# Branch products of a hybrid encoder layer: order of copies, splits and loads around them

## The chip, the cores and the metric

The kernel runs on one core of one Trainium2 chip, as one program. The metric is the device time of the program in microseconds. Three runs of the kernel before are known: 1832.99, 1835.6 and 1838.12 us, so the median is 1835.6 us. One more execution was profiled.

## The reference, cut to what matters

One layer on 512 frames of 2048 channels, all in float32. After a layer norm, one projection feeds three attention branches and their gates:

```
branches = (oa * silu(ag), ob * silu(bg), oc * silu(cg))        # each 512 x 1024
for n in range(3):
    gate = sigmoid(mg[..., n*2048:(n+1)*2048] + b_gate[n])      # 512 x 2048
    merged += gate * (branches[n] @ w_branch[n])                # 512 x 1024 @ 1024 x 2048
y = merged @ w_out
out = layer_norm(2**0.25 * h + y)
```

The change lies around the three products `branches[n] @ w_branch[n]`, and in one load of the last product `merged @ w_out`.

## The kernel before, in words

Every float32 product is made of three matmuls on parts of its operands. A value is split into a high part (ACT copies it to the format fp32r) and a low part (DVE subtracts the high part from the value); TensorE adds low x high, high x low and high x high in PSUM. Weights are split in the kernel as well, so each chunk of weights passes this way: SP issues its load into a slot of `raw` (4 slots of 512 KB), ACT writes `w_hi` (`split_hi`, L1262), DVE writes `w_lo` (`split_lo`, L1842), TensorE uses it (12 matmuls of 128x512), and the slot goes on. `split_hi(c)` and `split_lo(c)` work on chunk c + 3 (`LOOKAHEAD`); ACT waits in it until chunk c - 1 is multiplied, SP's load of a chunk waits until the low part of the chunk 4 before it is written.

**The gate groups** (L898 to L955, L1480, L2195) come before the branch products. In the last of them (group 7) DVE makes sums of weights in place of the weights (`weight_sum`, L2002). The fourth sum of a row of tiles is the last that reads `w_11`, which lies on the same bytes as `raw`. Behind group 7 the first chunks of the branch products are split between its last pieces (L1511, L2222).

**The branch products** use two forms. Branches 2 and 1 go through `halved_group` (L1141): 4 groups (s = 0 to 3), each one half of the columns of a branch, each with 7 products G1, G5, G6, G2, G7, G3, G4 in place of 8 (the Strassen-Winograd scheme), 2 chunks each, so 14 chunks a group. G5, G6, G7 and G4 take sums of weights that GpSimd's accumulating DMAs have made in DRAM (`t_dram`); the others take `w_branch` itself. The partial results stay in three pairs of PSUM banks, z, y and x. Before TensorE may start on a bank again something has to leave it: ACT copies z after G1, y after G5 and z after G6 (`copy_halved`, L1713, at steps j = 2, 4, 6); DVE adds x at j = 8, z at j = 10 and y at j = 12 (`add_out`, L2024). G6, G7 and G3 wait for the three copies, G4 for the add at j = 10, the next group for the other two (L1145 to L1157). DVE then multiplies by the gates (`halved_gates`, L2455, at j = 9, 11, 13; `halved_21`, L2473, at the next group's j = 0). ACT makes the tanh of two gate blocks a group (`gate_tanh`, L1708), which GpSimd loads from DRAM, 1 MB each (`load_gate`, L3027).

Branch 0 goes through plain products: 4 column blocks m of 4 chunks (L1171), with its own split tiles `bra_hi` and `bra_lo` (`branch_hi` L1475, `branch_lo` L2177), 8 tiles k of 128x512. TensorE needs tile k of them when it comes to the k-th of 8 parts of block m = 0.

The unsplit branches 1 and 0 come back from DRAM in one load of 2 MB each (`load_branch`, L2895), issued by GpSimd between its gate loads (L3040 to L3057). GpSimd issues in program order, so a load behind a wait waits too.

The order on ACT and DVE is written out by hand, step j by step j, as in

```python
                for j in range(STEPS):
                    split_hi(CH_M + STEPS * s + j)
                    ...
                    if j == 6:
                        copy_halved(s, 6, z, u2_buf, ev_u2, 6)
                        gate_tanh(2 * s)
```

**The output product** (L1201, L2692, L3070) uses the same scheme on `w_out`, with quarters of it in `w_x`, `w_y` and `w_z`. SP loads the quarters (`load_out`, L661); GpSimd adds further quarters into them with accumulating DMAs of 512 KB (`sum_out`, L3059), each as soon as the piece it overwrites is split. The order of TensorE's first pieces is G1 and G3, then G5 (from `w_x` after the adds), then G2 (from `w_z`, the third quarter), G6, G7, G4. SP issues the four loads of the third quarter once piece (G3, 1) is split (L674).

Of the kernel before, what the change touches and what calls it, by code (L numbers as in the profile page):

```python
# [31 lines left out]
D = 2048  # L32
# [6 lines left out]
BT = BW // P  # L39
# [15 lines left out]
RING = 4  # L55
# [13 lines left out]
CH_M = CH_A + 4 * PAIRS  # L69
# [28 lines left out]
SUMMED_C, SUMMED_B = 6, 8  # L98
SUMMED = 2 * (SUMMED_C + SUMMED_B)
LEFT_SUMS = 5  # L100
TOEP_DONE = 16 + 16 * PAIRS
# [9 lines left out]
def t_index(g, t, k):  # L111

    return 4 * BT * g + BT * (t - 1) + k
# [71 lines left out]
def program(nc, x, mem, ln_in_g, ln_in_b, rel_table, w_in, b_gate, b_forget, sinks,  # L185
# [205 lines left out]
    with ExitStack() as ctx:  # L391
# [146 lines left out]
        def _(sp):  # L538
# [107 lines left out]

            sp.wait_ge(t_ready, t_index(GROUPS, 1, 0))
            sp.wait_ge(toep_stored, TOEP_DONE + 16 * 8 * HALVED)
            for s in range(HALVED):
                for p in range(PRODUCTS):  # L650
                    src = t_dram[s, RIGHT[p]] if p in (G5, G6, G7, G4) else branch_weights(2 - s // 2, s % 2, RIGHT[p])
                    for h in range(2):
                        c = CH_M + STEPS * s + 2 * p + h
                        load(c, c % RING, src[2 * h * P:2 * (h + 1) * P, :].rearrange("(k p) n -> p k n", p=P), 2)
            for m in range(D // 512):
# [9 lines left out]
            def split_done(g, p, d):  # L665
                sp.wait_ge(pc_lo, OUT_BASE + double(g, p, d) + 1)
# [5 lines left out]
            for d in range(DOUBLES):  # L672
                load_out("22", w_y, 0, 1, 1, d)
            split_done(0, G3, 1)  # L674
            for d in range(DOUBLES):
# [585 lines left out]
        def _(act):  # L1261
# [197 lines left out]
            def halved_hi(b, p):  # L1459

                if p in (G5, G6, G7, G3):
                    made_at = {G5: 1, G7: 2, G6: 3, G3: 5}[p]
                    act.wait_ge(m_summed, LEFT_SUMS * b + made_at)
                else:
                    act.wait_ge(br_loaded[2 - b], 16)
                if b:
                    act.wait_ge(multiplied, CH_M + STEPS + 2 * p + 2)
                elif p in (G5, G6, G3):
                    act.wait_ge(pc_lo, piece(GROUPS - 1, G4, 2 * (G5, G6, G3).index(p) + 2))
                else:  # L1470
                    act.wait_ge(pc_mult, piece(GROUPS - 1, G4, 0))
                pick = branch_tiles(p)
                act.activation(pick(br_hi, bs_hi), pick(br_raw[b], bs_raw[b]), ACT.Copy).then_inc(br_hi_ready, 1)

            def branch_hi(k):  # L1475

                act.wait_ge(br_loaded[0], 16)
                act.activation(bra_hi[:, k, :], bra_raw[:, k, :], ACT.Copy).then_inc(br_hi_ready, 1)
# [240 lines left out]
            for s in range(HALVED):  # L1719
                z, y, x = gate_banks(GROUPS + s)  # L1720
                for j in range(STEPS):
                    split_hi(CH_M + STEPS * s + j)
                    if s == 0 and j < 4:
                        halved_hi(0, G2 + j)
                    if s == 0 and j == 6:
                        act.wait_ge(st_c12, 16 * GROUPS)
                    if j == 2:
                        copy_halved(s, 2, z, p1_buf, ev_s1, 2)
                    if j == 4:
                        copy_halved(s, 4, y, p5_buf, ev_s5, 4)  # L1730
                    if j == 6:
                        copy_halved(s, 6, z, u2_buf, ev_u2, 6)
                        gate_tanh(2 * s)
                    if j == 8:
                        gate_tanh(2 * s + 1, -0.5)
                    if s == 1 and j and j % 2 == 0:
                        halved_hi(1, j // 2 - 1)
                    if s == 2 and j == 0:
                        halved_hi(1, G4)
                    if s == 3 and j >= 12:  # L1740
                        branch_hi(j - 12)

            last_m = D // 512 - 1
            for m in range(last_m + 1):
                for s in range(4):
# [3 lines left out]
                    split_hi(CH_PLAIN + 4 * m + s)  # L1749
                    if m == 0 and s < 3:  # L1750
                        branch_hi(2 * s + 2)
                        branch_hi(2 * s + 3)
                    if s == (0 if m else 2):
# [87 lines left out]
        def _(dve):  # L1841
# [304 lines left out]
            def halved_sum(b, n):  # L2146
# [4 lines left out]
                if n:  # L2151
                    dve.wait_ge(m_summed, LEFT_SUMS * b + n)
                else:
                    dve.wait_ge(br_loaded[2 - b], 16)
                if n == 0:
# [329 lines left out]
            for s in range(HALVED):  # L2485
                g = GROUPS + s
                z, y, x = gate_banks(g)
                for j in range(STEPS):
                    if j == 10:
                        job_done(CH_M + STEPS * s + 9)  # L2490
                        dve.wait_ge(ev_s5, 2 * g + 2)
                        add_out(z, p5_buf, ev_c22)
                    split_lo(CH_M + STEPS * s + j)
                    if s == 0 and j < 5:
# [4 lines left out]
                    if s and j == 0:  # L2499
                        halved_21(s - 1)  # L2500
                    if j == 8:
                        job_done(CH_M + STEPS * s + 7)
                        dve.wait_ge(ev_s1, 2 * g + 2)
                        add_out(x, p1_buf, ev_c11)
                    if j == 9:
                        dve.wait_ge(ev_c11, 2 * g + 2)
                        halved_gates(s, 0, 0, p1_buf, 1.0)
                    if j == 11:
                        dve.wait_ge(ev_c22, 2 * g + 2)
                        halved_gates(s, 1, 1, p5_buf, -1.0)  # L2510
                    if j == 12:
                        job_done(CH_M + STEPS * s + 11)
                        dve.wait_ge(ev_u2, 2 * g + 2)
                        add_out(y, u2_buf, ev_c12)
                    if j == 13:
# [6 lines left out]
                    if s == 2 and j in (1, 2, 3, 4):  # L2522
                        halved_lo(1, G2 + j - 1)
                    if s == 3 and j >= 12:
                        branch_lo(j - 12)

# [56 lines left out]
            for m in range(last_m + 1):  # L2583
                for s in range(4):
# [3 lines left out]
                    if m == 0 and s == 0:  # L2588
                        halved_21(HALVED - 1)
                    if m == 0 and s < 3:  # L2590
                        branch_lo(2 * s + 2)
                        branch_lo(2 * s + 3)
                    if m == last_m - 1 and s == 1:
# [197 lines left out]
        def _(pool):  # L2791
# [103 lines left out]
            def load_branch(n, dst):  # L2895
                if n == N_BRANCH - 1:
                    pool.wait_ge(br_stored, 16 * (HC + 2 * PAIRS))
                pool.dma_start(dst, br_dram[n].rearrange("k p n -> p k n")).then_inc(br_loaded[n], 16)

            def store_gate(g, half_n, half_t, buf, done):  # L2900
                n, nb = N_BRANCH - 1 - (g - KV_GROUPS) // 2, 2 * (g % 2) + half_n
# [142 lines left out]
            store_gate(GROUPS - 1, 0, 1, s1_buf, st_c21)  # L3044
            load_gate(1)
            pool.wait_ge(multiplied, CH_M + 4)
            load_branch(1, br_raw[1][:, :, :])
            for done in (st_c11, st_c22, st_c21):
                pool.wait_ge(done, 16 * GROUPS)
            for m in range(2, 6):  # L3050
                load_gate(m)
            pool.wait_ge(multiplied, CH_M + 2 * STEPS + 6)
            load_branch(0, bra_raw[:, :, :])
            for m in range(6, 2 * HALVED + D // 512):
                load_gate(m)
                if m >= 2 * HALVED:
                    pool.dma_start(out_t[m - 2 * HALVED], ln_b[0].partition_broadcast(P)).then_inc(preset, 16)  # L3057
# [120 lines left out]
```

## Time and profile before

| | us |
|---|---|
| three runs | 1832.99, 1835.6, 1838.12 |
| the profiled execution, its own time | 1833.84 |
| its span, first to last instruction | 1832.1 |
| TensorE busy | 1807.1 |
| VectorE (DVE) busy | 1345.8 |
| ScalarE (ACT) busy | 902.7 |
| GpSimd busy | 240.6 |
| mean granted TensorE clock, share of full | 0.997 |

Times in the profile are microseconds from the first instruction. A matmul of 512 columns is shown as 0.39 us long, but the next starts 0.227 us after it; its end is modelled, and it overlaps the next. What TensorE loses is therefore read from the distance of starts, or from the idle time in brackets. Group 7's G4 runs from 1394 to 1406.6 us, the four groups of the branch products from 1406.8 to 1562.9, the plain products of branch 0 from 1565 to 1661, the output product from there to 1819.

### The profile page before, as it was taken

How to read it: one execution, taken by the hardware profiler on the slowest of the kernel's cores; microseconds unless marked ns; L12 is line 12 of the kernel's file. 1: busy time of each engine (PE TensorE's matmuls, PEld its weight loads, DVE VectorE, ACT ScalarE, POOL GpSimd, SP SyncE). 2: the span in 40 equal slices, each digit the busy share in tenths (PEclk: the TensorE clock that was granted, in tenths of full speed). 3: DMA queues.
4: the chain of work that ended last, by engine and by line, in shares of the span. 5: the costliest groups of instructions: out<-in, count | busy, mean ns of one | idle time of the engine just before them, and what ended most of it. 6: DMA issues, size and time to landing. Idle time of an engine off the chain costs nothing.

```text
span 1832.1 us, 24225 instructions
## 1 busy us (share of the span) xinstructions
PE 1807.1 (99%) x8481; PEld 1496.9 (82%) x8481; DVE 1345.8 (73%) x2130; ACT 902.7 (49%) x1504; POOL 240.6 (13%) x308
## 2 busy tenths in 40 slices
PE   9999999999999999999999999999999999999997
PEld 7888888888888888888888888888887887787885
DVE  5777774887777776566678877878788777656778
ACT  5653332545555554344445545545456575344543
POOL 1111110100222221001101110101111000002222
PEclk9999999999999999999999999999999999999999
DMA  9576676962765544355566967858787877739987
GB/s 329 184 204 176 188 199 208 247 218 59 197 199 151 180 130 141 110 154 158 122 191 179 263 152 193 234 124 235 182 229 184 313 258 251 247 133 201 240 209 178
DMA packets 249640, 354.98 MB, mean 194 GB/s; under 512 B 14480, under 2 KB 141520, under 8 KB 245968
## 3 DMA queue, kind: packets, MB, share of 16 engines
q1 hardware_dynamic: 178352, 200.83, 34.6%
q0 software_dynamic: 71056, 152.50, 34.3%
q8 instruction: 50, 0.82, 0.2%
q10 hardware_dynamic: 144, 0.52, 0.1%
q14 instruction: 38, 0.31, 0.1%
HBM read 303.30 MB, written 97.11 MB: 219 GB/s over the span
## 4 chain that ended last, share of the span: by engine, by line
PE 87%; DVE 5%; DMA 4%; ACT 1%; issue 1%; POOL 0%; DVEq 0%; POOLq 0%; SPq 0%; ACTq 0%
PE acc L715 10%; PE acc L717 10%; PE acc L716 10%; PE scores L906 6%; PE scores L910 6%; PE scores L908 6%; PE acc L910 3%; PE acc L906 3%; PE acc L908 3%; PE transposed L740 3%; DMA raw_weights<-anch_weight_sums_scratch 2%; PE attended L910 2%; PE attended L906 2%; PE attended L908 2%; DVE w_lo L1853 2%
## 5 line engine op out<-in xcount | busy, mean ns | idle before, releaser
L1380 ACT ACTIVATE piece_split<-w 128x512 fp32r<-128x512 f32 x448 | 282.5, 632 | 289.8 <-PE scores L910 105.6
L1999 DVE TENSOR_TENSOR piece_split<-w,piece_split 128x512 fp32r<-128x512 f32 x448 | 309.2, 691 | 108.3 <-ACT piece_split L1380 97.8
L1853 DVE TENSOR_TENSOR w_lo<-raw_weights,w_hi 128x1024 fp32r<-128x1024 f32 x205 | 249.3, 1221 | 149.8 <-ACT w_hi L1275 148.0
L715 PE MATMUL acc<-h_hi,w_lo 128*128 128x512 f32 x800 | 319.2, 399 | 0.0
L717 PE MATMUL acc<-h_hi,w_hi 128*128 128x512 f32 x800 | 312.5, 391 | 0.0
L716 PE MATMUL acc<-h_lo,w_hi 128*128 128x512 f32 x800 | 311.7, 390 | 0.0
L1275 ACT ACTIVATE w_hi<-raw_weights 128x1024 fp32r<-128x1024 f32 x205 | 216.1, 1059 | 158.1 <-PE acc L717 27.3
L717 PEld LDWEIGHTS acc<-h_hi,w_hi 128*128 128x128 f32 x800 | 150.1, 188 | 32.2
L715 PEld LDWEIGHTS acc<-h_hi,w_lo 128*128 128x128 f32 x800 | 150.4, 188 | 30.0 <-issue 1.8
L716 PEld LDWEIGHTS acc<-h_lo,w_hi 128*128 128x128 f32 x800 | 150.6, 188 | 28.5
L906 PE MATMUL scores<-piece_split,h_lo 128*128 128x512 f32 x384 | 150.2, 391 | 0.6 <-DVE piece_split L1999 0.3
L910 PE MATMUL scores<-piece_split,h_hi 128*128 128x512 f32 x384 | 149.4, 389 | 0.0
L908 PE MATMUL scores<-piece_split,h_hi 128*128 128x512 f32 x384 | 149.4, 389 | 0.0
L906 PE MATMUL acc<-piece_split,h_sums 128*128 128x512 f32 x256 | 99.6, 389 | 0.0
L908 PE MATMUL acc<-piece_split,h_sums 128*128 128x512 f32 x256 | 99.6, 389 | 0.0
L910 PE MATMUL acc<-piece_split,h_sums 128*128 128x512 f32 x256 | 99.6, 389 | 0.0
L906 PEld LDWEIGHTS scores<-piece_split,h_lo 128*128 128x128 f32 x384 | 72.1, 188 | 17.3 <-DVE piece_split L1999 2.8
L910 PEld LDWEIGHTS scores<-piece_split,h_hi 128*128 128x128 f32 x384 | 72.1, 188 | 15.0
L908 PEld LDWEIGHTS scores<-piece_split,h_hi 128*128 128x128 f32 x384 | 72.1, 188 | 14.8
L1561 ACT ACTIVATE b_probs_t_hi<-transposed 128x512 fp32r<-128x512 f32 (+1 forms) x64 | 24.5, 435 | 65.0 <-PE transposed L740 64.3
L908 PEld LDWEIGHTS acc<-piece_split,h_sums 128*128 128x128 f32 x256 | 48.1, 188 | 10.0
L910 PEld LDWEIGHTS acc<-piece_split,h_sums 128*128 128x128 f32 x256 | 48.1, 188 | 10.0
(490 smaller groups left out, 3716.2 us busy)
## 6 DMA issues: line engine op xcount, KB each, us to landing
w<-in_w_in SPq DMA_DIRECT2D x128, 512.0 KB, 9.4
raw_weights<-in_w_in SPq DMA_DIRECT2D x102, 512.0 KB, 4.0
anch_weight_sums_scratch<-in_w_branch POOLq DMA_DIRECT2D x24, 1024.0 KB, 10.2
raw_weights<-in_w_branch SPq DMA_DIRECT2D x40, 512.0 KB, 5.1
raw_weights<-in_w_mem_kv SPq DMA_DIRECT2D x32, 512.0 KB, 6.1
raw_weights<-anch_weight_sums_scratch SPq DMA_DIRECT2D x32, 512.0 KB, 4.6
gate_scratch<-in_b_gate POOLq DMA_DIRECT2D x12, 1024.0 KB, 12.3
gate<-gate_scratch POOLq DMA_DIRECT2D x12, 1024.0 KB, 8.9
```

Source lines behind the costliest of these rows:

```text
L715: pe.matmul(bank_out, wl, hi[:, k, :], start=first, stop=False)
L716: pe.matmul(bank_out, wh, lo[:, k, :], start=False, stop=False)
L717: return pe.matmul(bank_out, wh, hi[:, k, :], start=False, stop=last)
L740: last = pe.transpose(tp[f % 2][:, col:col + P], src, ident[:, :])
L906: pe.matmul(banks[t][:, :], lo[:, k, tok], wh, start=first and k == 0, stop=False, skip_group_check=True)
L908: pe.matmul(banks[t][:, :], hi[:, k, tok], wl, start=False, stop=False, skip_group_check=True)
L910: last = pe.matmul(banks[t][:, :], hi[:, k, tok], wh, start=False, stop=k == BT - 1, skip_group_check=True)
L1275: act.activation(w_hi[:, slot, :], raw[:, slot, :], ACT.Copy).then_inc(hi_ready, 1)
L1380: act.activation(p_split[:, n % RING, 0, :], sources[p][:, k, :], ACT.Copy).then_inc(pc_hi, 1)
L1561: act.activation(b_pth[:, k_off(kb):k_off(kb + 1)], tp[f % 2][:, 0:(TT - kb) * P], ACT.Copy).then_inc(b_pt_hi, 1)
L1853: dve.tensor_tensor(w_lo[:, slot, :], raw[:, slot, :], w_hi[:, slot, :].bitcast(F32), ALU.subtract).then_inc(lo_ready, 1)
L1999: dve.tensor_tensor(p_split[:, n % RING, 1, :], sources[p][:, k, :], p_split[:, n % RING, 0, :].bitcast(F32), ALU.subtract).then_inc(pc_lo, 1)
```

## The change

1. SP's first four chunk loads: each waits for the fourth weight sum of its own two rows of tiles, where the first waited for the sums of all eight; the wait for the weight sums in DRAM moves from before the first chunk to before the third (the first that reads them).
2. ACT, each group: the copies at j = 2, 4, 6 stand ahead of `split_hi` of the same step. The two gate tanh move from behind the copy at j = 6 and from j = 8 to behind the splits of j = 7 and j = 9.
3. DVE, each group: the adds at j = 8 and j = 12 stand ahead of `split_lo` of the same step (the add at j = 10 did already).
4. Branch 0's split: ACT's eight `branch_hi` from j = 12, 13 of group 3 and the first three steps behind it to j = 1 to 8 of group 3; DVE's `branch_lo` to j = 2 to 5 (four of them) and to the first two steps of block 0 (two each).
5. GpSimd: the loads of branches 1 and 0 in four parts of 512 KB, issued after 5, 7, 9 and 11 chunks of group 0 and of group 2; the second gate block of each group waits until 4 chunks of that group are multiplied. All who wait for branches 1 and 0 wait for all four parts.
6. SP: the third quarter of `w_out` is loaded once (G3, 3) is split, two pieces of G3 later.

```diff
+LOAD_PARTS = 4
@@ SP
-            sp.wait_ge(t_ready, t_index(GROUPS, 1, 0))
-            sp.wait_ge(toep_stored, TOEP_DONE + 16 * 8 * HALVED)
...
                         c = CH_M + STEPS * s + 2 * p + h
+                        if c < CH_M + RING:
+                            sp.wait_ge(t_ready, t_index(GROUPS - 1, 4, 2 * (c % RING) + 1) + 1)
+                        if (s, p, h) == (0, G5, 0):
+                            sp.wait_ge(toep_stored, TOEP_DONE + 16 * 8 * HALVED)
...
-            split_done(0, G3, 1)
+            split_done(0, G3, 3)
@@ ACT
-                    act.wait_ge(br_loaded[2 - b], 16)
+                    act.wait_ge(br_loaded[2 - b], 16 * (LOAD_PARTS if b else 1))
...
                 for j in range(STEPS):
-                    split_hi(CH_M + STEPS * s + j)
-                    if s == 0 and j < 4:
-                        halved_hi(0, G2 + j)
...
                         copy_halved(s, 6, z, u2_buf, ev_u2, 6)
+                    split_hi(CH_M + STEPS * s + j)
+                    if s == 0 and j < 4:
+                        halved_hi(0, G2 + j)
+                    if j == 7:
                         gate_tanh(2 * s)
-                    if j == 8:
+                    if j == 9:
                         gate_tanh(2 * s + 1, -0.5)
...
-                    if s == 3 and j >= 12:
-                        branch_hi(j - 12)
+                    if s == 3 and 0 < j <= BT:
+                        branch_hi(j - 1)
...
-                    if m == 0 and s < 3:
-                        branch_hi(2 * s + 2)
-                        branch_hi(2 * s + 3)
@@ DVE
+                    if j == 8:
+                        job_done(CH_M + STEPS * s + 7)
+                        dve.wait_ge(ev_s1, 2 * g + 2)
+                        add_out(x, p1_buf, ev_c11)
+                    if j == 12:
+                        job_done(CH_M + STEPS * s + 11)
+                        dve.wait_ge(ev_u2, 2 * g + 2)
+                        add_out(y, u2_buf, ev_c12)
                     split_lo(CH_M + STEPS * s + j)
...
-                    if s == 3 and j >= 12:
-                        branch_lo(j - 12)
+                    if s == 3 and 1 < j < 6:
+                        branch_lo(j - 2)
...
-                    if m == 0 and s < 3:
-                        branch_lo(2 * s + 2)
-                        branch_lo(2 * s + 3)
+                    if m == 0 and s < 2:
+                        branch_lo(2 * s + 4)
+                        branch_lo(2 * s + 5)
@@ GpSimd
+            def load_branch_rows(n, part, dst):
+                rows = slice(part * BT // LOAD_PARTS, (part + 1) * BT // LOAD_PARTS)
+                pool.dma_start(dst[:, rows, :], br_dram[n, rows].rearrange("k p n -> p k n")).then_inc(br_loaded[n], 16)
...
-            load_gate(1)
-            pool.wait_ge(multiplied, CH_M + 4)
-            load_branch(1, br_raw[1][:, :, :])
-            for done in (st_c11, st_c22, st_c21):
-                pool.wait_ge(done, 16 * GROUPS)
-            for m in range(2, 6):
+            for m in range(1, 2 * HALVED + D // 512):
+                s = m // 2
+                if m == 2:
+                    for done in (st_c11, st_c22, st_c21):
+                        pool.wait_ge(done, 16 * GROUPS)
+                if s < HALVED and m % 2:
+                    pool.wait_ge(multiplied, CH_M + STEPS * s + 4)
                 load_gate(m)
-            pool.wait_ge(multiplied, CH_M + 2 * STEPS + 6)
-            load_branch(0, bra_raw[:, :, :])
-            for m in range(6, 2 * HALVED + D // 512):
-                load_gate(m)
+                if m in (1, 5):
+                    for n in range(LOAD_PARTS):
+                        pool.wait_ge(multiplied, CH_M + STEPS * s + 5 + 2 * n)
+                        load_branch_rows(1 - s // 2, n, (bra_raw, br_raw[1])[m == 1])
```

## Rows read from the trace of the kernel before

**Rows 1.** The page's part 1: busy us (share of the span) and instructions.
```profile
PE 1807.1 (99%) x8481; PEld 1496.9 (82%) x8481; DVE 1345.8 (73%) x2130; ACT 902.7 (49%) x1504; POOL 240.6 (13%) x308
```

**Rows 2.** Who TensorE waited for: us in total, times, longest us.
```profile
PE scores L1189 <- DVE branch_a_lo L2180: 4.2, 3, 1.9
PE acc L1212 <- DVE out_piece_split L2580: 3.0, 1, 3.0
PE scores L1133 <- DVE branch_fifth_product L2026: 1.4, 2, 1.2
PE scores L1133 <- ACT second_sum L1388: 0.8, 1, 0.8
```

**Rows 3.** TensorE's timeline: start us, us, engine, line, op, xcount, [idle before, releaser].
```profile
1399.38 0.39 PE L910 MATMUL attended<-piece_split,h_hi 128*128 128x512 f32 x1
...
1406.81 0.39 PE L1133 MATMUL scores<-w_hi,branch_lo 128*128 128x512 f32 x1
...
1428.34 0.39 PE L1137 MATMUL attended<-w_hi,branch_hi 128*128 128x512 f32 x1
...
1562.72 0.39 PE L1137 MATMUL attended<-w_hi,branch_hi 128*128 128x512 f32 x1
...
1573.34 0.47 PE L1189 MATMUL scores<-w_hi,branch_a_lo 128*128 128x512 f32 x1 [1.17 <-DVE branch_a_lo L2180]
...
1689.28 0.39 PE L1216 MATMUL acc<-out_piece_split,merged_s 128*128 128x512 f32 x1
...
1696.64 0.39 PE L1214 MATMUL acc<-out_piece_split,merged_s 128*128 128x512 f32 x1
```

**Rows 4.** ACT's timeline around the stalls, same columns.
```profile
1397.74 1.06 ACT L1275 ACTIVATE w_hi<-raw_weights 128x1024 fp32r<-128x1024 f32 x1 [2.69 <-DMA raw_weights<-in_w_branch]
...
1427.49 1.06 ACT L1275 ACTIVATE w_hi<-raw_weights 128x1024 fp32r<-128x1024 f32 x1 [2.95 <-DMA raw_weights<-anch_weight_sums_scratch]
1428.46 1.07 ACT L1388 ACTIVATE second_sum<-scores 128x512 f32<-128x512 f32 x2
...
1558.31 0.61 ACT L1478 ACTIVATE branch_a_hi<-branch_a_unsplit 128x512 fp32r<-128x512 f32 x1
```

**Rows 5.** DVE's timeline: a weight sum, an add, a low part.
```profile
1374.31 0.69 DVE L2017 TENSOR_TENSOR w<-w,w 128x512 f32<-128x512 f32 x1
...
1517.27 1.29 DVE L2026 TENSOR_TENSOR branch_fifth_product<-scores,branch_fifth_product 128x512 f32<-128x512 f32 x2
...
1543.19 1.23 DVE L1853 TENSOR_TENSOR w_lo<-raw_weights,w_hi 128x1024 fp32r<-128x1024 f32 x1 [5.52 <-ACT w_hi L1275]
```

**Rows 6.** Timelines of SP's queue and of GpSimd: the DMA issues.
```profile
1390.41 0.88 SPq L544 DMA_DIRECT2D raw_weights<-in_w_branch  x2
...
1489.96 1.49 POOL L3037 DMA_DIRECT2D gate<-gate_scratch  x2 [37.15 <-DVE merged_rows L2452]
1501.35 0.89 POOL L2898 DMA_DIRECT2D branch_a_unsplit<-branch_scratch  x1 [9.91 <-PE scores L1137]
```

**Rows 7.** A window: us, busy of PE, PEld, DVE, ACT, POOL, PEclk, DMA share, GB/s.
```profile
1489.00:1512.00 23.00, 23.00 (x104) 19.02 (x102) 15.30 (x15) 13.73 (x15) 2.38 (x3) 1.00 0.96 338
```

**Rows 8.** DMA issues between 1501 and 1502.4 us: KB each, median us to landing.
```profile
branch_a_unsplit<-branch_scratch POOLq DMA_DIRECT2D x1, 2048.0 KB, 12.6
```

**Rows 9.** DMA issues in stretches at 1657, 1676, 1671.2 and 1672.8 us, in turn.
```profile
out_w_x<-in_w_out POOLq DMA_DIRECT2D x1, 512.0 KB, 6.0
...
out_w_x<-in_w_out POOLq DMA_DIRECT2D x1, 512.0 KB, 14.0
...
out_w_z<-in_w_out SPq DMA_DIRECT2D x1, 512.0 KB, 6.5
...
out_w_z<-in_w_out SPq DMA_DIRECT2D x1, 512.0 KB, 16.6
```

**Rows 10.** ACT's timeline and a window of the output product.
```profile
1690.23 1.06 ACT L1691 ACTIVATE out_piece_split<-out_w_x 128x1024 fp32r<-128x1024 f32 x1 [9.02 <-DMA out_w_x<-in_w_out]
...
1690.00:1700.00 10.00, 7.31 (x25) 5.90 (x26) 8.68 (x9) 9.77 (x12) 3.23 (x3) 0.83 1.12 203
```

More of the change, by code:

```diff
@@ L1475, in branch_hi @@
             def branch_hi(k):
-                act.wait_ge(br_loaded[0], 16)
+                act.wait_ge(br_loaded[0], 16 * LOAD_PARTS)
                 act.activation(bra_hi[:, k, :], bra_raw[:, k, :], ACT.Copy).then_inc(br_hi_ready, 1)
@@ L2153, in halved_sum @@
                 else:
-                    dve.wait_ge(br_loaded[2 - b], 16)
+                    dve.wait_ge(br_loaded[2 - b], 16 * (LOAD_PARTS if b else 1))
                 if n == 0:
@@ L2500, in _ @@
                         halved_21(s - 1)
[L2501 to L2504, printed above, removed]
                     if j == 9:
@@ L2510, in _ @@
                         halved_gates(s, 1, 1, p5_buf, -1.0)
[L2511 to L2514, printed above, removed]
                     if j == 13:
```

## The prediction, made before the change was run

> **What bounds the kernel now.** I read the page's busy shares first: TensorE is busy for 1807.1 us, 99% of the span, DVE for 73%, ACT for 49% [rows 1]. So an engine made faster, or work taken off one, brings nothing by itself; only the places where TensorE stands still can be won. The list of its waits names them, and nearly all lie where the change works: 4.2 us in three waits of the plain products for `branch_a_lo`, 3.0 us in one of the output product, 1.4 and 0.8 us in the halved groups [rows 2].
>
> A wait costs more than its idle time (refill, a lower clock), so I count by starts. The first 96 matmuls of the branch products run without a gap: (1428.34 - 1406.81)/95 = 0.2266 us from start to start [rows 3]. Against that pace:
> - **T1, end of gate group 7:** 25 starts from 1399.38 to 1406.81 take 7.43 us in place of 5.67: 1.8 lost.
> - **T2, halved groups:** 671 starts from 1406.81 to 1562.72 take 155.9 in place of 152.1: 3.8 lost.
> - **T3, first plain chunk:** 25 starts from 1562.72 to 1573.34 take 10.6 in place of 5.7: 4.9 lost.
> - **T4, output product, piece (G5, 2):** 11 starts from 1689.28 to 1696.64 take 7.4 in place of 2.5: 4.9 lost [all rows 3].
>
> Together 15.4 us, 0.84% of the run. That is the ceiling of this change; the product count on TensorE stays as it is.
>
> **T1, SP's first chunks (edit 1).** ACT stood idle for 2.69 us until the first chunk had landed, split it from 1397.74 on [rows 4], and the last pieces of G4 queued behind that split. SP had issued the load at 1390.41 [rows 6], after the last weight sum. The new wait is for the sum of rows 0 and 1, which DVE writes at 1374.31 [rows 5] and ends at 1375.0: 15 us earlier, more than any landing of 512 KB in my rows needs (6.0 to 16.6 us, rows 9; at 16.6 it lands at 1391.6, before ACT asks at 1395.05). SP has nothing else queued there, and only the third chunk waits for the sums in DRAM. ACT and DVE still have three chunk splits and branch splits between the pieces: on DVE a piece (0.69) and a chunk (1.22) are 1.9 us per piece against 6 x 0.2266 = 1.36, a lag of 0.5 a piece over three or four pieces, about 2 us, which the four piece slots (5.4 us) hide. Bounds 0.8 to 1.8; I take 1.6, since the wait named is the whole of ACT's delay.
>
> **T2, copies, adds and loads (edits 2, 3, 5).** At 1427.49 ACT had waited 2.95 us for a chunk's DMA, and only then, at 1428.46, copied the banks on which TensorE stood [rows 4]. G6 had ended a whole product (24 matmuls, 5.4 us) before the wait began. Ahead of the split the copy needs only the multiply, so that stall (0.8 plus about 0.3 for the refill) goes wholly. The other stalls are DVE's add into `branch_fifth_product` at j = 10, which already stood first in its step: it came late (1517.27, rows 5) because DVE's chain behind ACT had waited for chunks. The reason is in the transfers: both gate blocks of group 2 are issued together at 1489.96, 2 MB of branch 0 at 1501.35 [rows 6], the DMA engines are busy 0.96 of that stretch [rows 7], and the 2 MB take 12.6 us [rows 8]. The change spreads these 4 MB from 1490 to about 1515 (second gate after 4 chunks, parts after 5, 7, 9 and 11, a chunk being 12 x 0.2266 = 2.72 us), and the tanh no longer stand ahead of the next split. The demand (1 chunk per 2.72 us) is unchanged, so some lateness may remain. Bounds 1.1 (the copy alone) to 3.8; I take 3.3, as j = 10 was late by less than 1.3 us each time and both edits pull it forward.
>
> What this adds: six more loads on GpSimd, 0.9 us each, hidden (13% busy, rows 1). Behind its new waits stand the next gate loads, which wait later anyway (1489.96 after 37.15 us of waiting, rows 6). The wait for all four parts is the one to watch. Group 2 starts near 1484.5 on the old clock; part 4 is issued 11 chunks later, 1514.4, and lands between 1520 and 1531 by the ends 6.0 and 16.6 [rows 9]. ACT wants it at j = 1 of group 3, near 1525, and may be two chunks (5.4 us) late before TensorE notices. Cost 0, at worst 1 us. Branch 1 is the same, a group earlier, with DVE's first sum behind it. A copy ahead of a split delays that split by 1.07 (rows 4), an add by 1.29 (rows 5); the chunk split there is due three chunks, 8 us, later. Cost 0.
>
> **T3, branch 0's split (edit 4).** TensorE waits three times for `branch_a_lo` because its first high part was made at 1558.31 only [rows 4] and the low parts stood in DVE behind adds and gate products of up to 2.6 us each. After the change four of the eight are ready some 25 us early, and the k-th is needed k x 2.72 us into the block: DVE has 10.9 us for the fifth. Work moved, not added: 8 x 0.61 and 8 x 0.69 us into a group where ACT and DVE waited 5.5 us for one chunk (1543.19, rows 5). Behind T3 the next limit is the add at j = 12, now ahead of its split, due 5.4 us before the block begins. Bounds 3.5 to 4.9; I take 4.8.
>
> **T4, third quarter (edit 6).** ACT stood 9.02 us until 1690.23 for the accumulated half of `w_x` [rows 10]. The last accumulating load into it took 14.0 us, where one issued at 1657 took 6.0; between them SP had put four plain loads of the third quarter in, the last of which took 16.6 [rows 9]. Issued after (G3, 3), near 1680, they come 9 us later; the accumulating load issued at 1676.2 then lands near 1683, with half a collision at 1685, and must land before 1689.5 - 1.0 - 1.2 = 1687 (split times of rows 4 and 5). The new risk is G2, which reads the third quarter: it starts four doubles after (G5, 0), near 1695, its first two loads are due at 1692.5, and land at 1686.5 if they take 6.5 [rows 9], at 1696.7 if they take 16.6. The stretch after the wait ran at a mean clock of 0.83 [rows 10], that is, some starts at 1.2 GHz; of the 4.9 us about 1.6 are that.
>
> The Trainium skill (TensorE: Matmul & The Clock Gate, Part 1) says the clock is low by default and activity holds it up; by it the 1.6 go with the wait, without it they stay and T4 brings 3.3. The trace agrees so far as the low stretch follows the longest wait.
>
> Bounds of T4 -2.0 (a late G2 in place of G5, with its own refill) to 4.9; I take 4.2: the 6.0 us row is the nearest.
>
> **Sum.** 1.6 + 3.3 + 4.8 + 4.2 = 13.9 us off the profiled execution's own 1833.84 gives 1819.9. The median of the runs lies 1.8 above that execution, so I forecast 1835.6 - 13.9 = 1821.7 us.
>
> **Rivals.**
> - **R1, the collision is only moved (T4 brings nothing).** For it: the DMA engines stay full around 1690, and the same bytes have to pass; two more accumulating loads (G6) come in the same stretch. Against it: 9 us between the deadlines. Time 1821.7 + 4.2 = 1825.9, with a small G2 stall up to 1828. The Trainium skill (DMA: Bandwidth & Descriptors, Queues, rings and completion order) says each DMA engine takes turns between the queues that have work; by that rule the postponed loads take their share from the G6 sums instead, and only deadlines decide. The 14.0 beside 16.6 agrees.
> - **R2, the chunks stay late (T2 mostly stays).** For it: DMA at 0.96 [rows 7], the second gate block only some 5 us later. Against it: the copy doesn't depend on it. 1821.7 + 2.2 = 1823.9; with R1 1828.
> - **R3, slower: the lead of the chunk ring is used up.** In each of four groups three copies and three adds come ahead of, or hold up, a chunk's split: 24 places at 1.07 to 1.29 us. If chunks land just in time, each is a stall on `w_lo`: up to 24 x 1.2 = 28 us, against 13.9 won; it decides from 12 of the 24 on. For it: in group 3 the chunk split at 1543.19 [rows 5] was ready at 1544.4, and TensorE wanted it 71 starts before 1562.72, at 1546.6 or a little earlier: a lead under 2.2 us. Against it: TensorE never waited for `w_lo` in these groups [rows 2], and that chunk was late after double gate loads. All 24: 1835.6 + 28 - 15.4 = 1848.
> - **R4, no effect.** The releasers are inferred; if something behind them (a later DMA) sets each stall, they come back under new names: 1831 to 1836.
>
> **How the numbers follow.** Forecast 0.62, R1 0.16 and R2 0.09 (with both at once), R4 0.08, R3 0.05. A measurement of this kernel tells 0.3%, 5.5 us, from no change (its three runs spread over 5.1). Faster by more holds for the forecast, R1 and R2, less a little for spread: 0.84; within 0.3%: 0.11; slower: 0.05. The range runs from the ceiling, 1835.6 - 15.4 = 1820.2, less 3 for the spread of a median, 1817, to R1 and R2 together with 1 us more, 1829.
>
> **What would show it.** Right: ACT's first chunk split of group 0 follows its piece with no DMA idle; no `<-ACT second_sum` among TensorE's waits; the adds at j = 10 end before G4; no wait at the first plain chunk, 25 starts in 5.7 us; the accumulating load of `w_x` lands in 6 to 9 us and 11 starts of (G5, 2) take 2.5 us at full clock. Wrong: waits of TensorE for `w_lo` in the halved groups (R3), for `out_piece_split` at G2 (R1), or ACT idle for `branch_a_unsplit` at the start of group 3.

## The result, and the profile after

| | before | after |
|---|---|---|
| median of the runs beside each other (4 and 4), us | 1835.7 (1833.0 to 1838.1) | 1819.3 (1819.2 to 1820.3) |
| ratio, 95% interval | | 0.9912 [0.9895, 0.9929] |
| the profiled execution, its own time | 1833.84 | 1819.27 |
| its span | 1832.1 | 1817.4 |
| starts lost at T1, T2, T3, T4 | 1.8, 3.8, 4.9, 4.9 | 0.0, 0.05, 0.0, 0.0 |

The forecast was 1821.7 with a range of 1817 to 1829; the kernel became 16.4 us faster (13 to 19 by the interval), 14.6 from one profiled execution to the other. The product count and its pace are the same: the page's part 1 of the kernel after answers [rows 1], with 5 us less of TensorE and nearly nothing else.

```profile
PE 1802.1 (99%) x8481; PEld 1496.7 (82%) x8481; DVE 1345.6 (74%) x2130; ACT 904.4 (50%) x1504; POOL 244.9 (13%) x314
```

TensorE's list of waits after, against [rows 2], from 1100 us on (the branch work, the output product and what stands before them). `branch_a_lo`, `out_piece_split`, `branch_fifth_product` and `second_sum` are all gone; one group is left, and it is no row of the change.

```profile
PE scores L909 <- DVE piece_split L2000: 0.6, 2, 0.4
```

TensorE's timeline after at the same five marks as [rows 3], with the one stall that is new ahead of them. From 1400.24, 25 starts to 1405.90 (T1); 671 starts to 1558.00 (T2); 25 starts to 1563.66 (T3); from 1679.48, 11 starts to 1681.98 (T4). At 0.2266 us a start each stretch is full to 0.05 us.

```profile
1332.33 0.50 PE L909 MATMUL scores<-piece_split,h_lo 128*128 128x512 f32 x1 [0.37 <-DVE piece_split L2000]
...
1400.24 0.39 PE L913 MATMUL attended<-piece_split,h_hi 128*128 128x512 f32 x1
...
1405.90 0.39 PE L1136 MATMUL scores<-w_hi,branch_lo 128*128 128x512 f32 x1
...
1558.00 0.39 PE L1140 MATMUL attended<-w_hi,branch_hi 128*128 128x512 f32 x1
...
1563.66 0.39 PE L1192 MATMUL scores<-w_hi,branch_a_lo 128*128 128x512 f32 x1
...
1679.48 0.39 PE L1219 MATMUL acc<-out_piece_split,merged_s 128*128 128x512 f32 x1
...
1681.98 0.39 PE L1217 MATMUL acc<-out_piece_split,merged_s 128*128 128x512 f32 x1
```

So all 15.4 us of the ceiling came back. The profiled executions differ by 14.6 because the one of after has 0.65 us of new loss at 1332.33 and 0.12 at 1103, both before anything of the change acts (over the executions of the experiments the first varies from 0 to 0.6). The rest up to 16.4 is that the profiled execution before lay 1.9 us under its median, the one after on it; where the other executions before lost more isn't known.

ACT's timeline after answers [rows 4]: the first chunk (1395.82) follows its piece with no wait for a DMA, and in the halved groups the copy at j = 6 (`second_sum`) stands ahead of its chunk. In the output product ACT waits 2.02 us where it waited 9.02 [rows 10], and the longest wait is now for the third quarter.

```profile
1395.28 0.63 ACT L1383 ACTIVATE piece_split<-w 128x512 fp32r<-128x512 f32 x1 [0.73 <-PE acc L913]
1395.82 1.05 ACT L1278 ACTIVATE w_hi<-raw_weights 128x1024 fp32r<-128x1024 f32 x1
...
1422.48 1.09 ACT L1391 ACTIVATE second_sum<-scores 128x512 f32<-128x512 f32 x2 [0.93 <-PE scores L1140]
1423.46 1.06 ACT L1278 ACTIVATE w_hi<-raw_weights 128x1024 fp32r<-128x1024 f32 x1
...
1673.44 1.07 ACT L1694 ACTIVATE out_piece_split<-out_w_x 128x1024 fp32r<-128x1024 f32 x1 [2.02 <-DMA out_w_x<-in_w_out]
...
1685.38 1.06 ACT L1694 ACTIVATE out_piece_split<-out_w_z 128x1024 fp32r<-128x1024 f32 x1 [3.26 <-DMA out_w_z<-in_w_out]
```

ACT's waits for chunks in the halved groups, 1406 to 1560 us, after (total, times, longest). Before, the same two groups were 23.5 us in 13 waits, up to 4.7.

```profile
ACT w_hi L1278 <- DMA raw_weights<-in_w_branch: 5.0, 5, 1.7
ACT w_hi L1278 <- DMA raw_weights<-anch_weight_sums_scratch: 1.4, 3, 1.0
```

The transfers behind that, timelines of GpSimd and SP after against [rows 6]: gates and parts apart, and the third quarter issued at 1670.29, behind the accumulating load of 1666.36.

```profile
1493.40 0.75 POOL L3042 DMA_DIRECT2D gate<-gate_scratch  x1 [6.28 <-PE acc L1140]
1496.12 0.71 POOL L2903 DMA_DIRECT2D branch_a_unsplit<-branch_scratch  x1 [1.97 <-PE scores L1140]
...
1512.44 0.72 POOL L2903 DMA_DIRECT2D branch_a_unsplit<-branch_scratch  x1 [4.73 <-PE acc L1140]
...
1666.36 1.17 POOL L3067 DMA_DIRECT2D out_w_x<-in_w_out  x1 [0.49 <-DVE out_piece_split L2581]
...
1670.29 1.99 SPq L665 DMA_DIRECT2D out_w_z<-in_w_out  x4
```

The landings after against [rows 8, 9]: parts of branch 0 at 1497 to 1514, the accumulating load of 1666.36, and the last three of the four plain loads (KB each, median us to landing).

```profile
branch_a_unsplit<-branch_scratch POOLq DMA_DIRECT2D x3, 512.0 KB, 6.9
...
out_w_x<-in_w_out POOLq DMA_DIRECT2D x1, 512.0 KB, 7.1
...
out_w_z<-in_w_out SPq DMA_DIRECT2D x3, 512.0 KB, 10.1
```

Windows of the kernel after over (G5, 2) and over the stretch of [rows 10]: granted clock 1.00 in both (0.83 before), with the DMA engines as full as before. The stretch of [rows 7] stands at 0.91 in place of 0.96.

```profile
1488.00:1511.00 23.00, 23.00 (x103) 19.07 (x102) 16.61 (x18) 15.68 (x17) 2.88 (x4) 1.00 0.91 324
...
1679.00:1684.00 5.00, 5.00 (x23) 4.13 (x22) 5.00 (x5) 3.12 (x5) 1.19 (x1) 1.00 1.10 255
1690.00:1700.00 10.00, 10.00 (x46) 8.29 (x45) 8.04 (x11) 6.59 (x10) 1.93 (x3) 1.00 1.08 211
```

### The profile page after: what moved, and what is told of

The parts are those of the page before. It is cut to its first block, busy times and chain, and to the rows that moved or that the text cites. A ratio compares the mean times of both kernels' runs of the same rounds, so it can differ in the third digit from the quotient of the medians.

```text
span 1817.4 us, 24234 instructions
## 1 busy us (share of the span) xinstructions
PE 1802.1 (99%) x8481; PEld 1496.7 (82%) x8481; DVE 1345.6 (74%) x2130; ACT 904.4 (50%) x1504; POOL 244.9 (13%) x314
## 4 chain that ended last, share of the span: by engine, by line
PE 96%; DMA 2%; DVE 1%; issue 0%; ACT 0%; POOL 0%; DVEq 0%; POOLq 0%; SPq 0%; ACTq 0%
PE acc L718 10%; PE acc L720 10%; PE acc L719 10%; PE scores L909 6%; PE scores L911 6%; PE scores L913 6%; PE acc L909 3%; PE acc L911 3%; PE acc L913 3%; PE transposed L743 3%; PE attended L909 2%; PE attended L911 2%; PE attended L913 2%; DMA w<-in_w_in 2%; PE scores L1138 1%; PE scores L1136 1%
## 5 line engine op out<-in xcount | busy, mean ns | idle before, releaser
L913 PEld LDWEIGHTS scores<-piece_split,h_hi 128*128 128x128 f32 x384 | 72.1, 188 | 15.1
```

The costliest lines, as they stand in the source:

```text
L913: last = pe.matmul(banks[t][:, :], hi[:, k, tok], wh, start=False, stop=k == BT - 1, skip_group_check=True)
```

## Experiments

Each is the kernel after with one edit, but for the seventh. "Lost" is counted by starts in the profiled execution, as in the prediction. It carries more than the difference of two medians, since medians this close lie within each other's intervals. The experiments were timed at other times than the kernel after, with medians of 1835.4 to 1837.0 us for the kernel before beside them, so two medians that differ by 1 us or so say nothing.

**1. First chunks late again.**

```diff
+            sp.wait_ge(t_ready, t_index(GROUPS, 1, 0))
+            sp.wait_ge(toep_stored, TOEP_DONE + 16 * 8 * HALVED)
             for s in range(HALVED):
...
-                        if c < CH_M + RING:
-                            sp.wait_ge(t_ready, t_index(GROUPS - 1, 4, 2 * (c % RING) + 1) + 1)
```

> The changed kernel with edit 1 alone undone: SP's first chunk load waits for all weight sums again. Theory (T1 comes from that load): ACT idles 2 to 3 us for the first chunk's DMA, 25 starts at the end of gate group 7 lose 1.6 to 1.8 us again, all else stays, time +1.7 us against the changed kernel. Rival (the pieces were late by DVE's load, and another edit cured them): no more than 0.3 us lost there.

Measured: 1821.2 us (ratio to before 0.992 [0.990, 0.994]); T1 loses 2.2, the others nothing. ACT's wait for the first chunk is back, and a late piece behind it:

```profile
1398.29 1.06 ACT L1276 ACTIVATE w_hi<-raw_weights 128x1024 fp32r<-128x1024 f32 x1 [3.12 <-DMA raw_weights<-in_w_branch]
```

```profile
1400.64 0.50 PE L907 MATMUL scores<-piece_split,h_lo 128*128 128x512 f32 x1 [0.77 <-DVE piece_split L1998]
```

**2. ACT's copies behind the splits again, tanh at their old places.**

```diff
                 for j in range(STEPS):
+                    split_hi(CH_M + STEPS * s + j)
...
                         copy_halved(s, 6, z, u2_buf, ev_u2, 6)
-                    split_hi(CH_M + STEPS * s + j)
```

> The changed kernel with edit 2 alone undone: ACT's copies behind the split of their step and the tanh in their old places. Theory (copies behind late chunks made the stalls): one or two waits of TensorE for the copy of second_sum come back, 0.5 to 1.5 us. Rival (the chunks were late only because of the loads, which edit 5 has spread): at most 0.2 us lost in the halved groups.

Measured: 1820.0 us (0.991 [0.989, 0.993]), T2 loses 0.04. That is the rival's case: with chunks on time the order on ACT makes no difference.

**3. DVE's adds at j = 8 and 12 behind the splits again.**

```diff
-                    if j == 12:
-                        job_done(CH_M + STEPS * s + 11)
-                        dve.wait_ge(ev_u2, 2 * g + 2)
-                        add_out(y, u2_buf, ev_c12)
                     split_lo(CH_M + STEPS * s + j)
```

> The changed kernel with edit 3 alone undone: DVE's adds at j = 8 and j = 12 behind the split of their step. Theory of the prediction: the add at j = 12 ends before block 0 begins in either order and the one at j = 10, on which TensorE waited, stands where it stood, so at most 0.5 us comes back. Rival (DVE's order made the stalls at G4): 1 to 2.5 us lost in the halved groups.

Measured: 1819.5 us (0.992 [0.990, 0.993]); T2 0.05, T3 0.6, at the first plain start, where the add at j = 12 ended 0.1 us before TensorE began (1.5 us before in the kernel after). It is indeed the next limit there. But its order is only part of that: in experiments 5 and 6, with the add ahead of its split, 0.3 and 0.4 us went at the same start in the same way, since DVE came to the add late.

**4. Branch 0's split back at j = 12, 13 and in block 0.**

```diff
-                    if s == 3 and 0 < j <= BT:
-                        branch_hi(j - 1)
+                    if s == 3 and j >= 12:
+                        branch_hi(j - 12)
```

(and `branch_lo` likewise)

> The changed kernel with edit 4 alone undone: branch 0 is split at j = 12, 13 and in block 0 again. Theory (T3 is the order of this split): three waits at the head of block 0, 4 to 5 us lost in 25 starts. Rival (DVE was late there because of chunks and adds before it, which the other edits have moved forward): under 3 us lost.

Measured: 1823.3 us (0.993 [0.991, 0.994]); T3 loses 4.7, and the profiled execution 1.5 more at (G2, 2). TensorE's list of waits:

```profile
PE scores L1192 <- DVE branch_a_lo L2184: 4.0, 3, 1.7
PE transposed L1215 <- DVE out_piece_split L2584: 1.3, 1, 1.3
```

The second is the third quarter. Its loads were issued from 1674.99 on, and its third piece was split 19 us later (ACT's timeline): the stall of rival R1. Loads 3 and 4 count on one semaphore (`pc_loaded`), so the third piece waits for the fourth load as well, and that one landed at 1694.0, 17.0 us after its own issue.

```profile
1694.04 1.06 ACT L1694 ACTIVATE out_piece_split<-out_w_z 128x1024 fp32r<-128x1024 f32 x1 [3.12 <-DMA out_w_z<-in_w_out]
```

**5. GpSimd's loads as before: one of 2 MB, gates in pairs.** The diff is the GpSimd part of the change, backwards, with `LOAD_PARTS = 1`.

> The changed kernel with edit 5 alone undone: both gate blocks of a group together, branches 1 and 0 in one load of 2 MB at the old places. Theory (late chunks made DVE late): the waits for the add at j = 10 come back in groups 1 to 3, 1 to 2.5 us. Rival (the new order on ACT and DVE alone absorbs late chunks): ACT idles for chunks as before, 2 to 4.7 us at a time, and TensorE loses under 0.3 us.

Measured: 1822.3 us (0.993 [0.991, 0.994]); T2 loses 2.65, T3 0.3, and 1.5 at the start of the output product. ACT waits 27.0 us for chunks again, up to 4.6. TensorE's list shows the add of j = 10 (in groups 0 and 2, not 1 to 3), and no `second_sum`, but one wait for `w_lo` in group 0, which is the sign of rival R3 and costs 0.6 by starts:

```profile
PE scores L1136 <- DVE branch_fifth_product L2027: 1.4, 2, 0.9
PE transposed L743 <- ACTq L1709: 1.0, 1, 1.0
PE acc L1136 <- DVE w_lo L1854: 0.3, 1, 0.3
```

Under the old loads the stages lose 3.8 - 2.65 = 1.1 us less with the new order than without it. That is a comparison of two single executions, with edits 2 and 3 both in place, and the same old groups lost 4.4 in experiment 7; the order was never changed alone under the old loads. What it shows is that the stall on `second_sum` (1.1 by starts) is gone. Under the new loads ACT's order is worth nothing (experiment 2): edits 2 and 5 overlap.

**6. Third quarter back behind (G3, 1).**

```diff
-            split_done(0, G3, 3)
+            split_done(0, G3, 1)
```

> The changed kernel with edit 6 alone undone: the third quarter of w_out is loaded behind (G3, 1) again. Theory (T4 is the collision of these loads with the accumulating ones): the accumulating load into w_x issued at about 1665 takes 13 to 15 us again, TensorE waits 3 us at (G5, 2), and a stretch at 1.2 GHz follows, 4.9 us lost in all. Rival (the stall depended on how the earlier stages had shifted the loads): under 2 us lost.

Measured: 1825.5 us (0.993 [0.992, 0.995]), the largest part. One wait, then some ten starts at 0.43 us, 6.8 lost in all, where 4.9 was expected; T3 loses 0.4. TensorE's timeline, and a window on it:

```profile
1683.87 0.76 PE L1215 MATMUL acc<-out_piece_split,merged_s 128*128 128x512 f32 x1 [4.25 <-DVE out_piece_split L2581]
...
1686.99 0.63 PE L1217 MATMUL acc<-out_piece_split,merged_s 128*128 128x512 f32 x1
1687.42 0.63 PE L1219 MATMUL acc<-out_piece_split,merged_s 128*128 128x512 f32 x1
```

```profile
1684.00:1688.00 4.00, 4.00 (x10) 3.13 (x11) 4.00 (x5) 4.00 (x6) 2.22 (x2) 0.50 1.13 205
```

**7. The kernel before with edit 6 alone.**

```diff
-            split_done(0, G3, 1)
+            split_done(0, G3, 3)
```

> The kernel before with edit 6 alone. Theory: T4 goes whole (4.9 us faster than before, 11 starts of (G5, 2) in 2.5 us at 2.4 GHz), T1 to T3 stay at 1.8, 3.8 and 4.9 us. Rival: the stall only moves, to G2 or G6.

Measured: 1829.9 us (0.997 [0.996, 0.998]); T4 loses nothing, T1 1.9, T2 4.4, T3 5.0, and 1.3 at the start of the output product. The edit works by itself.

**8. All chunk splits of the halved groups one step later.**

```diff
-                    split_hi(CH_M + STEPS * s + j)
+                    if s or j:
+                        split_hi(CH_M + STEPS * s + j - 1)
```

(and `split_lo` likewise)

> The changed kernel with every chunk split of the halved groups one step later on ACT and DVE (a lead of two chunks in place of three, 2.7 us less), which prices the slower rival of the prediction. If the lead is near used up: TensorE waits for w_lo in many of the 56 chunks, 5 us lost or more. If the lead of the changed kernel is ample: under 1 us lost, and only where a chunk's DMA is late (group 3, about chunk 8).

Measured: 1819.9 us (0.992 [0.990, 0.993]), nothing lost. With a lead of two chunks in place of three there is still room. R3 is out.

**9 and 10. The third quarter behind (G3, 2), and behind (G5, 1).**

```diff
-            split_done(0, G3, 3)
+            split_done(0, G3, 2)     # 9;  (0, G5, 1) in 10
```

> The changed kernel with the third quarter loaded behind (G3, 2), between the place before (G3, 1; 6.6 us lost at (G5, 2)) and the new one (G3, 3; nothing lost). It is issued 3 us after the old place and 6 us before the new. If the collision works by shares of the DMA engines, the accumulating load into w_x lands 1 to 4 us late: 1 to 4 us lost at (G5, 2), and with a short wait no stretch at 1.2 GHz. Rival (any plain load ahead of the accumulating ones costs the whole): 5 us or more.

> The changed kernel with the third quarter loaded behind (G5, 1), some 4 us later than its new place. In the changed kernel the last of its four loads landed 15 us after its issue and was split 3 us before TensorE came to (G2, 2). Theory (the collision is moved and its deadline is near, R1 of the prediction): 1 to 3 us lost at G2. Rival (the loads pass faster there, since fewer accumulating ones are left): nothing lost.

Measured: 1823.2 us (0.992 [0.991, 0.994]) and 1825.3 us (0.994 [0.992, 0.995]). The place of 9 was only 1.9 us after the old one, not 3. With the other two places, in the profiled execution of each:

| place | issued, us | G5 loses | G2 loses | median |
|---|---|---|---|---|
| (G3, 1) | 1662.3 | 6.8 | 0 | 1825.5 |
| (G3, 2) | 1664.2 | 3.9 | 0 | 1823.2 |
| (G3, 3), the change | 1670.3 | 0 | 0 | 1819.3 |
| (G5, 1) | 1673.7 | 0 | 6.2 | 1825.3 |

In 9 the accumulating load into `w_x` landed 13.0 us after its issue, 5.9 later than in the changed kernel, where I had expected 1 to 4. The wait was 1.97 us, and I had expected no low clock with so short a wait; TensorE's timeline and a window show it all the same:

```profile
1681.69 0.47 PE L1215 MATMUL acc<-out_piece_split,merged_s 128*128 128x512 f32 x1 [1.97 <-DVE out_piece_split L2581]
...
1683.59 0.63 PE L1215 MATMUL acc<-out_piece_split,merged_s 128*128 128x512 f32 x1
1684.02 0.63 PE L1217 MATMUL acc<-out_piece_split,merged_s 128*128 128x512 f32 x1
```

```profile
1682.50:1685.50 3.00, 3.00 (x9) 2.36 (x8) 3.00 (x5) 3.00 (x5) 1.30 (x2) 0.52 1.12 204
```

In 10 the stall has moved to G2, with its own low stretch, and costs 6.2 where 1 to 3 was expected. ACT's timeline:

```profile
1685.32 1.06 ACT L1694 ACTIVATE out_piece_split<-out_w_z 128x1024 fp32r<-128x1024 f32 x1 [7.88 <-DMA out_w_z<-in_w_out]
...
1693.61 1.06 ACT L1694 ACTIVATE out_piece_split<-out_w_z 128x1024 fp32r<-128x1024 f32 x1 [3.42 <-DMA out_w_z<-in_w_out]
```

**11. Gates apart, but branches 1 and 0 in one load each, at the first part's place.**

```diff
-LOAD_PARTS = 4
+LOAD_PARTS = 1
```

> The changed kernel with branches 1 and 0 in one load of 2 MB each, at the place of the first of the four parts; the gate blocks stay apart. If the four parts make the gain of edit 5: most of the 2.7 us in the halved groups comes back. If the gate blocks do: under 0.7 us.

Measured: 1821.7 us (0.992 [0.990, 0.994]); T2 loses 2.8, as with all of edit 5 undone, and 1.5 go at the start of the output product. TensorE's list:

```profile
PE scores L1136 <- DVE branch_fifth_product L2027: 2.1, 2, 1.8
```

**12. Four parts, but the gate blocks in pairs again.**

```diff
-                if s < HALVED and m % 2:
-                    pool.wait_ge(multiplied, CH_M + STEPS * s + 4)
```

> The changed kernel with the second gate block of a group issued right behind the first; branches 1 and 0 stay in four parts. If the four parts make the gain of edit 5: under 0.7 us lost in the halved groups. If the gate blocks do: most of 2.7 us comes back.

Measured: 1819.7 us (0.990 [0.989, 0.992]); T2 loses 0.04. ACT waits 16.6 us for chunks, 10 more than after, and none of it reaches TensorE. In the profiled execution 2.0 went at (G2, 2), where the third quarter was late once more:

```profile
PE transposed L1215 <- DVE out_piece_split L2581: 1.7, 1, 1.7
```

The four parts are what matters in edit 5. Whether it is their size or their spacing isn't shown: four parts issued back to back were not tried. No version beat the changed kernel by more than its spread (2, 3, 8 and 12 are level with it).

## Why the prediction was right, step by step

The time was 2.4 us under the forecast: 1.5 because all 15.4 of the ceiling came and not 13.9, less 0.8 of loss elsewhere, and some 1.8 because the forecast carried the distance of the profiled execution before from its median over to the kernel after, which has none. The first part is the prediction's own error; the last is the spread of executions, and nothing in the prediction foresaw it.

- **T1 (taken 1.6, came 1.8).** Undone alone it costs 2.2, with ACT's wait for the first chunk in it. The lag of DVE that I held back 0.2 for does not show.
- **T2 (taken 3.3, came 3.75).** The size was near, the split between the edits only half right. The step "Ahead of the split the copy needs only the multiply" holds under the old loads (no `second_sum` in experiment 5), but it isn't what clears the groups: with one load in place of four parts 2.8 us come back under the new order (11), and with the four parts the old order of ACT or of DVE costs nothing in these groups (2, 3; both undone together was not run). Setting the gates apart, which I counted into the spreading, brings nothing there (12). That the copies pull the add at j = 10 forward, as "both edits pull it forward" has it, doesn't show: with them in place and the old loads it stalled TensorE for 1.4 us in two waits (5), just as before [rows 2].
- **T3 (taken 4.8, came 4.9).** Undone 4.7, in the same three waits. The next limit behind it is the add at j = 12, as forecast: 0.6 with its old order (3), 0.3 and 0.4 with its new one when DVE was late (5, 6), nothing in the changed kernel.
- **T4 (taken 4.2, came 4.9).** The accumulating load was forecast near 1683 on the old clock; it landed at 1666.36 + 7.1 = 1673.5, which is 1683.3 there ((G5, 2) stands 9.8 us earlier after than before), so that step was right. The 0.7 held back for half a collision was not needed. The size of the stall isn't fixed either: undone in the changed kernel it costs 6.8, with a wait of 4.25 us where it was 3.0 [rows 2], and a longer low stretch. With the wait gone the stretch ran at a granted clock of 1.00, and T4 brought 4.9, not the 3.3 of a low stretch that stays. That agrees with what the Trainium skill says, that activity holds the clock up (TensorE: Matmul & The Clock Gate, Part 1).
- **What I costed at nothing.** The wait for four parts: ACT never waited for `branch_a_unsplit`, whose parts landed 4.8 to 8.7 us after issue. The delay of chunk splits by copies and adds: nothing in the changed kernel, with a lead one chunk shorter too (8), but 0.6 in one place under the old loads (5).
- **R1** is real but not in the median. The prediction looked only at the first two loads of the third quarter, due at 1692.5; the tight one is the third piece, which waits for loads 3 and 4. It was split at 1685.4, its low part was done at 1687.7, and TensorE came to it at 1690.6: 2.9 us to spare. From the first issue to the fourth landing took 15.1 to 19.0 us over the ten profiled executions with this place, and the two longest, experiments 4 and 12, lost 1.5 and 2.0 us there; in both SP also took longer to issue the four (2.6 and 3.7 us against 2.0). One place later, 6.2 us are lost. That this is near the 6.3 between R1's 1828 and the forecast is chance: R1 counted T4's 4.2 as lost and a small G2 stall on top, and here G5 loses nothing and G2 all of it. The accumulating load issued ahead of the quarter took 7.1 us, the one issued beside it 10.9, and with the quarter 3.4 us later (10) that one took 5.9. That agrees with the rule cited there from the Trainium skill (DMA: Bandwidth & Descriptors, Queues, rings and completion order).
- **R2** isn't seen (6.4 us of waits for chunks are left of 23.5), **R3** is refuted for the changed kernel by 8 (its sign appears once in 5, under the old loads), **R4** by undos 1, 4, 5 and 6, each of which brought its own stall back.

The single undos sum to 2.2 + 0 + 0.6 + 4.7 + 2.65 + 6.8 = 17.0 us against 15.4 together, each counted only at the stage that it was meant for.

**Open.** The start of the output product loses 1.3 to 1.5 us in three profiled executions (5, 7, 11). The trace names the transfer behind it: ACT stands 7.5 to 7.8 us in front of its first split of `w_y` and can't copy out the transposes of `merged`, on which TensorE waits. ACT's timelines of experiment 5 and of the kernel after:

```profile
1661.48 1.06 ACT L1694 ACTIVATE out_piece_split<-out_w_y 128x1024 fp32r<-128x1024 f32 x1 [7.77 <-DMA out_w_y<-in_w_out]
...
1656.74 1.06 ACT L1694 ACTIVATE out_piece_split<-out_w_y 128x1024 fp32r<-128x1024 f32 x1 [5.22 <-DMA out_w_y<-in_w_out]
```

The second of SP's four loads into `w_y` landed 7.7 to 7.9 us after its issue in these three and 5.3 to 6.5 us in all the others. All three kernels load the branches in one piece each; so does the kernel before, which shows no such stall, and why the landing is late stays open. Which of the landings of the third quarter will be late in an execution can't be told from these profiles either.

## What to carry to other kernels

Count what TensorE loses by starts, at each stall, and take the sum as the ceiling: here all but 0.05 us of it came back at the four stages, while the medians moved by 1 us more, within their spread. When a reordering and a spreading of transfers aim at the same stall, look for what made the engine's input late; with that cured ACT's order was worth nothing, and under the old loads the new order went with at most 1.1 of the 3.8 us. A load that can be moved has a deadline on both sides: write down the landing of the last load that each reader waits for, at the worst length in the trace (16.6 us before, 17.0 in experiment 4 and 18.2 in experiment 10), before choosing its place; here 6 us earlier cost 3.9, 3.4 us later 6.2, and the chosen place itself 1.5 and 2.0 in two executions of ten.

## What the runs showed of the hardware

- **A low-clock stretch follows some stalls and not others.** In the output product stalls of 2.35 (experiment 9), 3.41 (before), 3.49 (10) and 4.63 us (6) from start to start were each followed by some 3 us or more with starts at 0.43 us, the level of 1.2 GHz by the granted clock of 0.50 and 0.52 in the windows of experiments 6 and 9. A stall of 2.60 us in the halved groups (7) had none, nor had three of 2.34, 1.44 and 1.56 us within 9 us at the head of the plain products before, as this window on them shows (granted clock third from the end):

```profile
1565.00:1574.00 9.00, 6.72 (x27) 4.95 (x28) 9.00 (x14) 2.04 (x4) 1.11 (x2) 1.00 0.55 162
```

  So the length of the last stall alone doesn't tell, and a wait of 2 us can cost 3.9. What else decides wasn't tried.
- **An accumulating load takes twice as long behind plain loads.** The same 512 KB landed 7.1 us after issue ahead of the four plain loads, and 13.0 (experiment 9), 14.0 [rows 9] and 14.5 (experiment 6) behind them.
- **Four paced loads of 512 KB were worth 2.8 us over one of 2 MB** at the same place (experiment 11). From 1488 to 1511 us the DMA engines were busy 0.91 of the time against 0.95, and the chunk loads issued from 1485 to 1515 us landed in 7.3 us by the median (8.9 at most) against 9.0 (10.9). That the chunk loads come through between the parts is a reading of these numbers. The sum of ACT's waits doesn't tell what reaches TensorE: 20.4 us in 11 cost 2.8, 16.6 in 12 nothing.
